# First loads in halves, x behind the projections' weights, a query chunk ahead of the scores, and a sum and its bank moved in the FFN seams

## What is computed

```python
for i in range(DEPTH):                      # DEPTH = 2; i = 0 GLA mixer, i = 1 convolution mixer
    x = layer_norm(ALPHA * x + 0.5 * swiglu(x, ffn1_w_gu[i], ffn1_w_down[i]), ...)
    if i == 0: y, qm = gla_mix(x @ gla_w_in, ...)
    else:      y, qm = conv_mix(x @ conv_w_in, ...)
    k, v = split(mem @ mem_w_kv[i])         # mem_attention: 4 heads of 128
    m = softmax(qm k^T / sqrt(128)) v
    x = layer_norm(ALPHA * x + concat[y, m] @ w_out, ...)
    x = layer_norm(ALPHA * x + 0.5 * swiglu(x, ffn2_w_gu[i], ffn2_w_down[i]), ...)
```

## Time and profile before

| What | Value |
|---|---|
| median of 3 runs | 2138.03 us (2136.85 to 2140.4) |
| profiled execution, its own time | 2137.1 us |
| its span in the trace | 2135.2 us |
| PE busy | 2092.3 us, 98% of the span |
| share of PE in the chain that ended last | 88% |
| granted TensorE clock, mean | 0.991 |
| DMA | 238.22 MB, 112 GB/s mean |

### The profile page before, as it was taken

How to read it: one execution, slowest core, us unless ns; L and a number is a source line. 1 busy time by engine, 2 the same in 40 slices (tenths; PEclk the granted TensorE clock), 3 DMA queues, 4 the chain that set the end, 5 groups by cost and what they waited for, 6 DMA issues and landing times.

```text
span 2135.2 us, 27022 instructions
## 1 busy us (share of the span) xinstructions
PE 2092.3 (98%) x10917; PEld 1784.6 (84%) x10917; DVE 972.6 (46%) x1299; ACT 690.0 (32%) x940; POOL 238.0 (11%) x170
## 2 busy tenths in 40 slices
PE   8999999999999999999999999999999899999998
PEld 7888888888987988888898888889887698888887
DVE  2333333443435833333363433336899773333235
ACT  5322222263433343322233333214342433222213
POOL 4121000043313210000011000002000321000000
PEclk9999999999999999999999999999999899999999
DMA  6644322332212234433233343332533222222231
GB/s 214 224 138 157 98 75 90 112 101 79 67 34 79 95 114 138 157 118 101 93 113 125 132 148 116 101 109 97 198 141 130 85 74 95 92 90 87 81 109 58
DMA packets 207167, 238.22 MB, mean 112 GB/s; under 512 B 5679, under 2 KB 199341, under 8 KB 205036
## 3 DMA queue, kind: packets, MB, share of 16 engines
q1 hardware_dynamic: 206444, 234.89, 32.9%
q10 hardware_dynamic: 640, 2.16, 0.2%
HBM read 215.02 MB, written 22.02 MB: 111 GB/s over the span
## 4 chain that ended last, share of the span: by engine, by line
PE 88%; DVE 5%; ACT 3%; issue 2%; DMA 1%; POOL 1%; ACTq 0%; POOLq 0%; SPq 0%; DVEq 0%
PE bank L1429 23%; PE bank L1430 23%; PE bank L1431 23%; PE bank L1436 3%; PE bank L1437 3%; PE bank L1438 3%; DVE u L1366 2%; PE bank L1507 1%; ACT u L641 1%; PE bank L1791 1%; PE bank L1790 1%; PE bank L1789 1%; DVE u L1155 1%; PE bank L1512 1%; POOL xlo L454 1%
## 5 line engine op out<-in xcount | busy, mean ns | idle before, releaser
L547 ACT CAST whi<-raw 128x2048 fp32r<-128x2048 f32 (+3 forms) x194 | 330.1, 1702 | 1082.5 <-PE bank L1431 975.5
L957 DVE TENSOR_TENSOR wlo<-raw,whi 128x2048 fp32r<-128x2048 f32 (+2 forms) x168 | 342.9, 2041 | 584.9 <-ACT whi L547 574.0
L1429 PE MATMUL bank<-xhi,whi 128*128 128x512 f32 x1552 | 607.7, 392 | 0.0
L1430 PE MATMUL bank<-xlo,whi 128*128 128x512 f32 x1552 | 604.6, 390 | 0.0
L1431 PE MATMUL bank<-xhi,wlo 128*128 128x512 f32 x1552 | 604.5, 389 | 0.0
L1429 PEld LDWEIGHTS bank<-xhi,whi 128*128 128x128 f32 x1552 | 291.6, 188 | 62.5 <-issue 2.1
L1431 PEld LDWEIGHTS bank<-xhi,wlo 128*128 128x128 f32 x1552 | 291.7, 188 | 61.0
L1430 PEld LDWEIGHTS bank<-xlo,whi 128*128 128x128 f32 x1552 | 291.8, 188 | 60.2 <-issue 0.5
L1429 PE MATMUL bank<-h_hi,whi 128*128 128x512 f32 x528 | 208.0, 394 | 3.3 <-DVE wlo L957 3.3
L1431 PE MATMUL bank<-h_hi,wlo 128*128 128x512 f32 x528 | 205.5, 389 | 0.0
L1430 PE MATMUL bank<-h_lo,whi 128*128 128x512 f32 x528 | 205.5, 389 | 0.0
(11 more groups left out here) (296 smaller groups left out, 2910.9 us busy)
## 6 DMA issues: line engine op xcount, KB each, us to landing
raw<-in_ffn_w_gu_dram SPq DMA_DIRECT2D x88, 1024.0 KB, 4.9
raw<-in_ffn_w_down_dram SPq DMA_DIRECT2D x32, 896.0 KB, 4.4
raw<-in_ffn_w_down_dram SPq DMA_DIRECT2D x32, 512.0 KB, 3.4
raw<-in_gla_w_in_dram SPq DMA_DIRECT2D x14, 1024.0 KB, 5.1
raw<-in_conv_w_in_dram SPq DMA_DIRECT2D x10, 1024.0 KB, 5.3
early_raw<-in_conv_w_in_dram SPq DMA_DIRECT2D x18, 512.0 KB, 5.3
lo_scratch<-early_lo SPq DMA_DIRECT2D x18, 512.0 KB, 4.0
raw<-in_mem_w_kv_dram SPq DMA_DIRECT2D x8, 1024.0 KB, 6.0
```

The source lines that it names most:

```text
L547: nc.scalar.copy(whi[:, s, 0:kc, 0:width], raw[:, s, 0:kc, 0:width]).then_inc(hi_ready, 1)
L957: nc.vector.tensor_tensor(wlo[:, s, 0:kc, 0:width], raw[:, s, 0:kc, 0:width], whi[:, s, 0:kc, 0:width].bitcast(F32), ALU.subtract).then_in ...
L1429: nc.tensor.matmul(to, whi[:, s, k, w], hi, start=start, stop=False)
L1430: nc.tensor.matmul(to, whi[:, s, k, w], lo, start=False, stop=False)
```

## The change

The diff touches five places. **First loads:** `mem` and chunk 0 are loaded in halves, in turn; x is loaded in halves behind chunks 5 and 6, the parameters behind chunk 7, and the x transposes stand behind chunks 4 and 5, the parameters behind 6. **First stage:** ten matmuls of a tile of ones run on PE ahead of the first data; ACT casts `mem_hi` straight from the bank, DVE makes `mem_lo` from the bank instead of POOL, and chunk 0 is split in halves. **Values:** for the values' chunks `mem` is the stationary operand, so that they come out untransposed, and `kv_values` is gone with its four copies. **FFN seams:** the lo part of the second chunk of the next pair moves into the middle of `residual_pair`, and the last pair's second half goes to banks (6, 4) and waits for `y_evac` 2 instead of 6. **GLA entry:** DVE instead of ACT copies `a_t`, DVE instead of POOL splits the first query chunk, PE runs that chunk ahead of the scores, and ACT's exponentials move behind that chunk's copies.

```diff
-DOWN_BANKS = [(6, 7), (0, 1), (2, 3), ((0, 1), (2, 3))]
+DOWN_BANKS = [(6, 7), (0, 1), (2, 3), ((0, 1), (6, 4))]
 OUT_BANKS = [(0, 1), (2, 3), ((0, 1, 2, 3), (0, 1, 2, 3))]
...
-            sp.dma_start(mem_in[:, :, :], a["mem"][0].rearrange("(b p) d -> p b d", p=P)).then_inc(mem_loaded, 16)
-            for layer in range(DEPTH):
-                w = a["mem_w_kv"][layer].rearrange("(k p) n -> p k n", p=P)
-                for c in range(4):
-                    n = KV_N + 4 * layer + c
-                    load(n, n % 2, cols(w, c * 256))
-                    if n == 1:
-                        sp.dma_start(xin[:, :, :], a["x"][0].rearrange("(b p) d -> p b d", p=P)).then_inc(x_loaded, 16)
-                        load_parameters()
+            mem = a["mem"][0].rearrange("(b p) d -> p b d", p=P)
+            w0 = a["mem_w_kv"][0].rearrange("(k p) n -> p k n", p=P)
+            for i in range(2):
+                half = slice(4 * i, 4 * i + 4)
+                sp.dma_start(mem_in[:, :, i * 512:(i + 1) * 512], mem[:, :, i * 512:(i + 1) * 512]).then_inc(mem_loaded[i], 16)
+                sp.dma_start(raw[:, 0, half, :], w0[:, half, 0:256]).then_inc(raw_loaded[0] if i else first_loaded, 16)
+            x_rows = a["x"][0].rearrange("(b p) d -> p b d", p=P)
+            for n in range(1, 8):
+                w = a["mem_w_kv"][n // 4].rearrange("(k p) n -> p k n", p=P)
+                load(KV_N + n, n % 2, cols(w, n % 4 * 256))
+                if n in (5, 6):
+                    i = n - 5
+                    sp.dma_start(xin[:, :, i * 512:(i + 1) * 512], x_rows[:, :, i * 512:(i + 1) * 512]).then_inc(x_loaded[i], 16)
+            load_parameters()
             ffn(0)
...
-            for k in range(DK):
-                pool.wait_ge(mem_hi_ready, 2 * k + 2)
-                nc.gpsimd.tensor_tensor(mem_lo[:, k, :], kv_t[:, 0, k, :],
-                                        mem_hi[:, k, :].bitcast(F32), ALU.subtract).then_inc(mem_ready, 1)
             lo_of(0, range(DK), slice(0, SEQ), xlo, xhi)
...
-            with pool.Fori(0, 5) as i:
+            split_lo(GLA_N + 5, 1, after_dve=True)
+            with pool.Fori(1, 5) as i:
...
-                nc.scalar.copy(kv_t[:, 0, k, :], bank[4 + k % 4][:, 0:NMEM]).then_inc(mem_hi_ready, 1)
-                act.wait_ge(mem_hi_ready, 2 * k + 1)
-                nc.scalar.copy(mem_hi[:, k, :], kv_t[:, 0, k, :]).then_inc(mem_hi_ready, 1)
-                if k % 4 == 3:
-                    split_hi(0, k // 4)
+                nc.scalar.copy(mem_hi[:, k, :], bank[4 + k % 4][:, 0:NMEM]).then_inc(mem_hi_ready, 1)
+                if k in (3, 5):
+                    half = slice(0, 4) if k == 3 else slice(4, 8)
+                    act.wait_ge(first_loaded if k == 3 else raw_loaded[0], 16)
+                    nc.scalar.copy(whi[:, 0, half, :], raw[:, 0, half, :]).then_inc(first_hi if k == 3 else hi_ready, 1)
+            split_hi(0, 1)
...
-                    if n == 0 and t == 0:
-                        act.wait_ge(mem_ready, DK)
-                    nc.scalar.copy(kv_t[:, n // 4, 2 * (n % 4) + t, :], bank[2 * (n % 2) + t][:, 0:NMEM]).then_inc(kv_evac, 1)
-                if n < 2:
-                    x_part(4 * n)
-                if n == 2:
+                    c = n % 4
+                    to = kv_t[:, n // 4, 2 * c + t, :] if c < 2 else kv_v[:, n // 4, t, (c - 2) * 256:(c - 1) * 256]
+                    nc.scalar.copy(to, bank[2 * (n % 2) + t][:, 0:NMEM]).then_inc(kv_evac, 1)
+                if n in (4, 5):
+                    x_part(4 * (n - 4))
+                if n == 6:
                     act.wait_ge(tr_done, 2 * DK + 1)
...
-            for j in range(4):
-                act.wait_ge(kvv_done, j + 1)
-                nc.scalar.copy(kv_v[:, j // 2, j % 2, :], bank[4 + j][:, :]).then_inc(kvv_evac, 1)
-            act.wait_ge(kvv_evac, 4)
+            act.wait_ge(kv_evac, 16)
...
             step(2)
-            act.wait_ge(w_used, GLA_N + 4)
-            nc.scalar.copy(a_t, bank[4][0:2 * RANK, :]).then_inc(gla_evac, 1)
             step(3)
             gates()
-            exps_of(0, 0)
             for j in range(8):
                 if j < 6:
...
-                if j % 2:
+                if j == 0:
+                    exps_of(0, 0)
+                elif j % 2:
                     probs_back(0, j // 2)
-                elif j:
+                else:
                     mo_hi_copy(0, j // 2 - 1)
                     exps_of(0, j // 2)
...
-            def residual_pair(ln, p, n_used, coef, banks):
+            def residual_pair(ln, p, n_used, coef, banks, between=None):
 
                 for t in range(2):
                     d = 2 * p + t
+                    if t == 1 and between is not None:
+                        split_lo(*between)
                     if t == 1 and p:
                         add_square(ln, d - 1, 0)
...
-                        residual_pair(ln, p, n0 + 4 * p + 4, 0.5, DOWN_BANKS[p])
-                        split_lo(n0 + 4 * p + 5, 1, DOWN_K[1])
+                        residual_pair(ln, p, n0 + 4 * p + 4, 0.5, DOWN_BANKS[p], (n0 + 4 * p + 5, 1, DOWN_K[1]))
...
-            for n in range(10):
+            def mem_low(ks):
+                for k in ks:
+                    dve.wait_ge(mem_hi_ready, k + 1)
+                    nc.vector.tensor_tensor(mem_lo[:, k, :], bank[4 + k % 4][:, 0:NMEM], mem_hi[:, k, :].bitcast(F32),
+                                            ALU.subtract).then_inc(mem_ready, 1)
+
+            mem_low(range(4))
+            dve.wait_ge(first_hi, 1)
+            nc.vector.tensor_tensor(wlo[:, 0, 0:4, :], raw[:, 0, 0:4, :], whi[:, 0, 0:4, :].bitcast(F32),
+                                    ALU.subtract).then_inc(first_lo, 1)
+            mem_low(range(4, 6))
+            dve.wait_ge(hi_ready, 1)
+            nc.vector.tensor_tensor(wlo[:, 0, 4:8, :], raw[:, 0, 4:8, :], whi[:, 0, 4:8, :].bitcast(F32),
+                                    ALU.subtract).then_inc(lo_ready, 1)
+            mem_low(range(6, 8))
+            for n in range(1, 10):
                 split_lo(n, n % 2)
             ffn(0)
 
...
+            dve.wait_ge(w_used, GLA_N + 4)
+            nc.vector.tensor_copy(a_t, bank[4][0:2 * RANK, :]).then_inc(gla_evac, 1)
+            split_lo(GLA_N + 4, 0)
             gates()
...
                     if c == 0:
-                        pe.wait_ge(y_evac, Y_BASE[ln] + (6 if h else 4))
+                        pe.wait_ge(y_evac, Y_BASE[ln] + (2 if h else 4))
...
+            pe.wait_ge(consts, 1)
+            for _ in range(10):
+                nc.tensor.matmul(bank[0][:, 0:P], ones[:, :], ones[:, :], start=True, stop=True)
             pe.wait_ge(consts, 3)
-            pe.wait_ge(mem_loaded, 16)
             for k in range(DK):
+                if k % 4 == 0:
+                    pe.wait_ge(mem_loaded[k // 4], 16)
                 if k >= 4:
-                    pe.wait_ge(mem_hi_ready, 2 * (k - 4) + 1)
+                    pe.wait_ge(mem_ready, k - 3)
                 for b in range(MB):
...
-                pe.wait_ge(x_loaded, 16)
+                pe.wait_ge(x_loaded[k0 // 4], 16)
                 for k in range(k0, k0 + 4):
                     if k < 4:
-                        pe.wait_ge(mem_hi_ready, 2 * (k + 4) + 1)
+                        pe.wait_ge(mem_ready, k + 5)
...
             for n in range(8):
-                pe.wait_ge(lo_ready, n + 1)
+                if n:
+                    pe.wait_ge(lo_ready, n + 1)
                 if n >= 2:
                     pe.wait_ge(kv_evac, 2 * (n - 1))
-                for k in range(DK):
-                    if n == 0:
-                        pe.wait_ge(mem_ready, k + 1)
-                    for t in range(2):
-                        last = mm3(bank[2 * (n % 2) + t][:, 0:NMEM], n % 2, k, t, mem_hi[:, k, :], mem_lo[:, k, :], k == 0, k == DK - 1)
+                if n % 4 < 2:
+                    for k in range(DK):
+                        if n == 0:
+                            pe.wait_ge(mem_ready, k + 1)
+                            if k in (0, 4):
+                                pe.wait_ge(lo_ready if k else first_lo, 1)
+                        for t in range(2):
+                            last = mm3(bank[2 * (n % 2) + t][:, 0:NMEM], n % 2, k, t, mem_hi[:, k, :], mem_lo[:, k, :], k == 0, k == DK - 1)
+                else:
+                    for j in range(MB):
+                        to, rows = bank[2 * (n % 2) + j][:, 0:256], slice(j * P, (j + 1) * P)
+                        for k in range(DK):
+                            nc.tensor.matmul(to, mem_hi[:, k, rows], whi[:, n % 2, k, :], start=(k == 0), stop=False)
+                            nc.tensor.matmul(to, mem_hi[:, k, rows], wlo[:, n % 2, k, :], start=False, stop=False)
+                            last = nc.tensor.matmul(to, mem_lo[:, k, rows], whi[:, n % 2, k, :], start=False, stop=(k == DK - 1))
                 last.then_inc(w_used, 1)
-                if n < 2:
```

(19 more changed lines are left out.)

12 lines of the change are left out of this document (7 added, 5 removed).

## The result

The changed kernel takes **2115.2 us** (median of four runs, 2114.9 to 2118.6); beside it the kernel before took 2138.4. The ratio is 0.9895, with a 95% interval of 0.9878 to 0.9912: faster by 1.05%. Every part did what it was said to do, and their sum, 17.4 us, was too small.

A forecast was written before the change was run, and what follows sets the result against it. PE, busy 98% of the span, bounds the kernel; 6.2 + 1.7 + 8.3 + 1.2 = 17.4 us off the profiled 2137.1 gives 2119.7, and the median, 0.9 above, 2120.6 us; range 2116 to 2126.5.

The forecast's parts named there:

- first stage: Up to the first FFN: new loads and casts start that FFN at 61.7 instead of 67.90, 6.2 us less (4.8 to 7.6).
- values: The transposes of the values on PE go, saving 1.7 us.
- seams: At the FFN seams, PE's pauses for the lo part and the second residual go: 8.3 us, between 4 and 9.
- GLA entry: Gates 0.4 us sooner, and the query chunk fills the scores' wait of 0.85: together 1.2 us, between 0 and 2.
- 2.08 us a FFN, four times: In each FFN, pauses of 0.97 (third pair's second chunk) and 1.11 us (last pair's second half) go: 8.3 us.
- the later residual: In the FFNs, the second residual comes 1.2 us later behind the moved subtraction, which nobody on PE awaits.
- The seams give half: Rival: the later second residual delays the norm behind each down projection, so 0.97 or 1.11 returns; 2124.8 us, chance 0.12.
- So I take the middle: First stage: chunk 1 starts between 15.5 and 18.3, depending on the clock during chunk 0; 16.9 taken.
- the sum's lower bound: First stage: the earliest start of the first FFN, with the largest gain of the range, 7.6 us instead of 6.2.
- the clock stays low through chunk 0: Rival: in the first stage chunk 0 takes 8.56 us again, gain 4.8 instead of 6.2; 2122.0 us, chance 0.25.
- The rule on transposes: First stage: transposes not counting as busy would leave the clock low at chunk 0, the gain 1.4 us smaller.
- 4 us to spare: GLA entry: head 0's exponentials move back 2 us, and its transposes have 4 us to spare behind chunk 1.

The follow-up runs named there:

- second execution: The changed kernel measured again with no edit, its profiled execution at its median: 2114.8 us, ratio 0.9904 against the kernel before.
- first profile: The profiled execution of the changed kernel in the result's own measurement, no further edit: 2118.6 us, the longest of the four runs.

## Why the prediction was wrong

The second execution's 22.2 us against the 17.4 forecast, term by term:

| term | forecast | measured | from |
|---|---|---|---|
| first stage | 6.2 | 6.9 (5.9 in the other) | start of the first FFN |
| values | 1.7 | 1.8 | first `h_hi` matmul |
| seams | 8.3 | 10.2 | 2.5 per FFN; 10.2 by undoing them, rows; 11.5, medians |
| GLA entry | 1.2 | 1.2; 1.05 by undoing it | from 11.2 ahead of it to 12.4 at head 0's transposes; undone |
| elsewhere | 0 | 2.1 | the rest |

- **The step that failed is the seams'.** "2.08 us a FFN, four times" took the two pauses that the view of waits names. It missed the third, 0.25 us without a bracket, and what each restart adds: the start behind a pause comes 0.1 us late as well. The term measured 2.54 us a FFN; four times the missing 0.46 is the 1.9 us between 8.3 and 10.2. The mechanism was right: `wlo` and `u` went from the list as said, the moved subtraction had room, and the later residual (0.6 us against PE, not 1.2) delayed nobody. "The seams give half" did not happen. This step alone does not carry the time out of the range: with 10.2 in its place the forecast would have been 2118.7, and the result lies below that because of "Elsewhere" (2.1) and the first stage (0.7), too.
- **First stage.** The load order, the halves and the casts came as worked out: chunk 0 at 9.12 to 10.0 for 9.7. "So I take the middle", 16.9 for chunk 1, was too cautious: in the second execution the whole stage ran at the high level and chunk 1 started at 16.2, which its own lo part set. The FFN's 61.01 lies midway between the forecast, 61.7, and the sum's lower bound, 60.3. The rival "the clock stays low through chunk 0" is refuted as a rule and holds as an accident: in the first profile chunk 0 was partly at the lower level, which cost 1 us.
- **The rule on transposes.** By the Trainium skill ("TensorE: Matmul & The Clock Gate", Part 4, PE-mode transpose) transposes don't count as busy for the clock. The runs agree with half of it: 16 transposes without the ones before them, in two groups, stayed at 1.94 and 1.97 us per eight, the lower level. But behind ten matmuls of ones they took 1.07 and 1.09, and the clock was still high at chunk 0. And in the kernel before, 16 transposes without a pause ended with the clock at the high level, from 9.6 us; it fell only in the pause behind them. So the prediction misread: chunk 0 began low there because of the pause, not because transposes had left the clock low. The smaller gain that the rule was said to bring did not come.
- **Values and GLA entry** came out as worked, 1.8 for 1.7, and 1.05 to 1.2 for 1.2. What the prediction said of the transposes of head 0, "4 us to spare", was wrong in three of the profiles: with the clock full, DVE's scan meets POOL's subtraction, the reserve is gone, and PE waits 1.34 to 1.51 us.
- **Elsewhere.** Of the 2.1 us, 1.4 lie behind the last transposes: from their start to the end are 9.66 us before and 8.25 in the second execution, 9.35 in the first; the last output DMAs took 5.90 and 4.42. The rest, 0.8, is won in the conv mixer, where the stretches at the lower clock lie otherwise in the two executions. That neither belongs to the change is an inference: no edit touches these places, but of the kernel before there is only one profile. The forecast started from one profiled execution and had no term for these, and its range gave 2.4 us to them where single runs of the changed kernel alone differ by 3.7 (2114.9 to 2118.6). With a misjudged term of 1.9 on top, the lower end was too tight.
- The kernel before was measured at 2138.0 ahead of the forecast, and at 2138.4, 2135.4, 2137.2, 2137.1 and 2135.1 beside the groups: of the gain of 23.2 us in the result 20.6 are left in the second measurement. By the experiments first stage and values are worth 7.7 to 8.4 us, the seams 10.2 to 11.5, the GLA entry 1.05, 19 to 21 us together; the rest of the gain in the result is within the scatter of the two kernels.

## What to carry to other kernels

Where an engine is 98% busy, find its pauses by the distance from one start to the next, over the whole repeated pattern, and not by the view of waits: a pause that overlapping records hide, and the slower start behind a visible one, were a fifth of what the seams gave. When two waits stand one behind the other on the engine that feeds it, remove both or expect little: of two edits one alone gave 3 us, the other 1.5, and both over 10. And give a range the scatter of single profiled executions, since the rows come from one.
